# A fused transformer layer on one core: reordering the seam between the output projection and the routed experts

## The reference, cut to what matters

```python
h = rmsnorm(x, norm1_g) * (1 + sc1) + sh1                # the six vectors sh1 .. g2 come from SiLU(cond) @ w_mod + b_mod
p = h @ w_in                                             # two kinds of attention follow; o joins their heads
x = x + g1 * (o @ w_out)                                 # output projection, 2048 x 2048
h2 = rmsnorm(x, norm2_g) * (1 + sc2) + sh2
aff = softmax(h2 @ w_router)                             # 16 experts
gate, idx = top_k(aff.T, cap)                            # each expert picks 64 latent and 16 context tokens
xs = h2[idx]
out = (silu(xs @ w_gate[e]) * (xs @ w_up[e])) @ w_down[e] * gate
x = x + g2 * scatter_add(out, idx)
y = rmsnorm(x, final_norm_g)
```

## Time and profile before

| | |
|---|---|
| median of 3 runs | 2119.72 us (2118.65 to 2121.78) |
| the profiled execution's own time | 2122.72 us |
| its span in the profile | 2120.7 us |
| PE busy | 2033.6 us, 96% |
| DVE busy | 1140.4 us, 54% |
| ACT busy | 478.9 us, 23% |
| GpSimd busy | 162.5 us, 8% |
| DMA | 614.03 MB, mean 290 GB/s |
| mean granted TensorE clock | 0.985 of full speed |

### The profile page before, as it was taken

How to read it: one execution, slowest core, us unless ns; L and a number is a source line. 1 busy time by engine, 2 the same in 40 slices (tenths; PEclk the granted TensorE clock), 3 DMA queues, 4 the chain that set the end, 5 groups by cost and what they waited for, 6 DMA issues and landing times. The chain is left out here.

```text
span 2120.7 us, 37671 instructions
## 1 busy us (share of the span) xinstructions
PE 2033.6 (96%) x15045; PEld 1130.4 (53%) x15045; DVE 1140.4 (54%) x2672; ACT 478.9 (23%) x846; POOL 162.5 (8%) x237
## 2 busy tenths in 40 slices
PE   6999999999999999999969999999999999999994
PEld 3578888787878887888742333333333333333331
DVE  4369988997558877777155333332233333223314
ACT  4232222212257775222110000000000000000003
POOL 1020011111000001111030000000000000000001
PEclk9999999999999999999979999999999999999997
DMA  9956667563120006665379999999999999999997
GB/s 388 410 181 221 218 233 258 190 219 109 60 102 1 2 1 247 218 218 183 111 286 371 405 414 415 417 417 426 419 416 416 416 417 417 426 419 416 418 392 290
DMA packets 71956, 614.03 MB, mean 290 GB/s; under 512 B 8464, under 2 KB 10136, under 8 KB 29136
## 3 DMA queue, kind: packets, MB, share of 16 engines
q1 hardware_dynamic: 47392, 514.36, 58.8%
q0 software_dynamic: 18704, 84.89, 13.1%
q10 hardware_dynamic: 5776, 13.63, 1.8%
HBM read 583.28 MB, written 29.60 MB: 289 GB/s over the span
## 5 line engine op out<-in xcount | busy, mean ns | idle before, releaser
L1249 PE MATMUL ps<-arena 128*32 128x512 f32 x6144 | 664.2, 593 | 0.3 <-DVE arena L2304 0.3
L1249 PEld LDWEIGHTS ps<-arena 128*32 128x32 f32 x6144 | 199.6, 110 | 459.7 <-issue 459.2
L1276 PE MATMUL ps<-arena 128*32 128x512 f32 x3072 | 332.5, 592 | 1.8 <-DVE arena L2315 1.8
L697 PE MATMUL ps<-B_w_hi,B_x_hi 128*128 128x512 f32 x720 | 286.8, 398 | 5.7 <-DVE B_x_lo L2034 3.3
L699 PE MATMUL ps<-B_w_lo,B_x_hi 128*128 128x512 f32 x720 | 281.6, 391 | 0.0
L698 PE MATMUL ps<-B_w_hi,B_x_lo 128*128 128x512 f32 x720 | 281.3, 391 | 0.0
L1276 PEld LDWEIGHTS ps<-arena 128*32 128x32 f32 x3072 | 99.7, 110 | 231.9 <-issue 229.2
L2336 DVE COPY arena<-arena 128x16 f32 x1200 | 157.4, 182 | 100.2 <-issue 99.4
L2312 DVE TENSOR_TENSOR arena<-ps,arena 64x256 f32<-64x256 f32 x96 | 40.0, 417 | 295.4 <-ACT arena L1607 294.8
L1607 ACT ACTIVATE arena<-ps 64x512 f32<-64x512 f32 x48 | 28.6, 595 | 610.3 <-PE ps L1249 610.3
L697 PEld LDWEIGHTS ps<-B_w_hi,B_x_hi 128*128 128x128 f32 x720 | 135.6, 188 | 46.5 <-issue 13.4
(11 more groups left out here) (287 smaller groups left out, 1972.2 us busy)
## 6 DMA issues: line engine op xcount, KB each, us to landing
arena<-in_w_expert SPq DMA_DIRECT2D x192, 2048.0 KB, 13.2
arena<-in_w_in_b SPq DMA_DIRECT2D x36, 1024.0 KB, 5.0
arena<-in_w_mod_q SPq DMA_DIRECT2D x32, 1024.0 KB, 19.2
arena<-in_w_mod POOLq DMA_DIRECT2D x32, 1024.0 KB, 5.4
arena<-in_w_mod POOLq DMA_DIRECT2D x32, 512.0 KB, 4.5
arena<-in_w_out_b SPq DMA_DIRECT2D x16, 1024.0 KB, 6.6
arena<-in_w_mod POOLq DMA_DIRECT2D x64, 256.0 KB, 3.3
arena<-in_x_sample SPq DMA_DIRECT2D x8, 1024.0 KB, 10.4
```

Source lines behind the costliest of these rows:

```text
L697: eng.matmul(out, x_hi, w_hi, start=start, stop=False)
L1249: mm = pe.matmul(bank(g)[32 * q:32 * q + 32, :], e_rows, w[q], start=start, stop=stop, skip_group_check=True)
L1276: mm = pe.matmul(bank(b)[32 * q:32 * q + 32, :], hT[g][:, f, :], w_four[q], start=f == 0, stop=f == 7, skip_group_check=True)
```

## The change

Four edits, all in the seam:

1. The fourth late sum on PE moves from behind block 25 to behind block 26 (LATE_SUM_AT). DVE's copy of the sums out of bank 7 moves from i == 31 to i == 28 and waits for fewer logits. PE's wait for that copy moves from router(3, 0), behind block 31, to router(2, 0), behind block 29.
2. DVE clears its tables at i == 30, ahead of residual(3), instead of behind it. It also writes two small tables (gateC's and idxC's context parts) behind the token numbers instead of ahead of them.
3. ACT alternates squares and copies of the last column block strictly: squares(3, t), take_raw of tile t. Before, the copy was two tiles behind.
4. x1_d gets 16 more columns and holds the factors beside the rows; rstd_d goes. One indirect DMA fetches 2064 columns instead of two that fetch 2048 and 16.

```diff
-LATE_SUM_AT = {7: 0, 13: 1, 19: 2, 25: 3}
+LATE_SUM_AT = {7: 0, 13: 1, 19: 2, 26: 3}
...
-        x1_d = nc.dram_tensor("x1_d", [TOK, D], F32, kind="Internal").ap()
-        rstd_d = nc.dram_tensor("rstd_d", [TOK, ROW_PAD], F32, kind="Internal").ap()
+        x1_d = nc.dram_tensor("x1_d", [TOK, D + ROW_PAD], F32, kind="Internal").ap()
...
                     for pair in ROUTER_AT.get(h, ()):
+                        if (n, pair) == (3, 0):
+                            pe.wait_ge(g2_ready, 1)
                         router(n - 1, pair)
             for t in range(NT):
                 raw_transposes(3, t)
                 if t == 2:
-                    pe.wait_ge(g2_ready, 1)
                     router(3, 0)
...
             for t in range(NT):
                 squares(3, (t,))
-                if t >= 2:
-                    take_raw(3 * NT + t - 2)
-            for t in range(NT - 2, NT):
                 take_raw(3 * NT + t)
...
-            act.wait_ge(gathered, 32)
+            act.wait_ge(gathered, 16)
...
-                pool.dma_start(rstd_d[P * t:P * (t + 1), :], rstdP[:, t, :]).then_inc(r_stored, 16)
+                pool.dma_start(x1_d[P * t:P * (t + 1), D:D + ROW_PAD], rstdP[:, t, :]).then_inc(r_stored, 16)
...
-            for cols, rows in ((slice(0, D), x1_d), (slice(D, D + ROW_PAD), rstd_d)):
-                pool.indirect_dma_start(xs[0:CAP, cols], None, rows[:, :],
-                                        bass.IndirectOffsetOnAxis(ap=idxC[:, 0:1], axis=0)).then_inc(gathered, 16)
+            pool.indirect_dma_start(xs[0:CAP, :], None, x1_d[:, :],
+                                    bass.IndirectOffsetOnAxis(ap=idxC[:, 0:1], axis=0)).then_inc(gathered, 16)
...
-                if i == 31:
+                if i == 28:
                     dve.wait_ge(late_summed, 4)
-                    dve.wait_ge(logits_done, 3 * NT)
+                    dve.wait_ge(logits_done, 2 * NT)
                     dve.tensor_copy(g2rows, bank(7)[:, 3 * P:4 * P]).then_inc(g2_ready, 1)
+                if i == 30:
+                    link(dve.memset(aff32[:, :, :], -1.0))
+                    for m, (a0, v) in enumerate(((0, 0), (2 * NE * 2, 0), (0, 1))):
+                        sel = ident[:, a0:a0 + 4 * NE].rearrange("p (c v e) -> p v e c", c=2, v=2)[:, v]
+                        ins = dve.tensor_reduce(by_kind[:, m, :], sel, AX, ALU.add)
+                    link(ins)
+                    dve.memset(logits_T[64:P, 2 * P:3 * P], 0.0)
                 if h == 7:
                     residual(n)
...
-            link(dve.memset(aff32[:, :, :], -1.0))
...
             dve.tensor_scalar(idxC[CL:CAP, 0:NE], bank(2)[CL:CAP, 0:NE], float(LAT - P), None, ALU.add)
-            dve.tensor_copy(gateC[CL:CAP, :], bank(2)[CL:CAP, NE:2 * NE])
-            dve.tensor_scalar(idxC[0:CX, NE:NE + 1], bank(2)[0:CX, 3 * NE - 1:3 * NE], -float(P), None, ALU.add)
...
             dve.tensor_copy(idxC[0:CL, 0:NE], later).then_inc(cols_ready, 1)
+            dve.tensor_copy(gateC[CL:CAP, :], bank(2)[CL:CAP, NE:2 * NE])
+            dve.tensor_scalar(idxC[0:CX, NE:NE + 1], bank(2)[0:CX, 3 * NE - 1:3 * NE], -float(P), None, ALU.add)
```

More of the change, by code:

```diff
@@ L2407, in _ @@
             dve.wait_ge(con_taken, NE + 1)
-            dve.wait_ge(gathered, 48)
+            dve.wait_ge(gathered, 32)
             for h, taken, at_least in ((0, half_taken, NE), (1, y_taken, NE + 1)):
```

## The result

| | before | after |
|---|---|---|
| median | 2119.72 us (5 runs, 2118.65 to 2121.85) | 2109.13 us (5 runs, 2108.68 to 2110.88) |
| ratio | | 0.9948, 95% interval 0.9937 to 0.9960 |
| profiled execution, its span | 2122.72, 2120.7 us | 2108.68, 2106.9 us |

A forecast was written before the change was run, and what follows sets the result against it. PE was taken to set the pace, so gains in the seam reach the end: -4.3 - 4.1 - 0.6 = -9.0 us, from the profiled 2122.72 to 2113.7, as a median 2110.7; range 2106.5 to 2116.0.

The forecast's parts named there:

- The late sum: Behind block 25: moving the fourth sum behind block 26 removes PE's 2.79 us wait and the half clock; -4.3 us.
- The copy of g2rows and PE's new wait: DVE's copy at i == 28, PE's wait behind block 29: costs nothing, with 13 us of cover.
- The last residual: Around block 31's end: DVE starts it earlier, ACT becomes the limit at 1.30 us a tile, logits come sooner; -4.1 us.
- a rival of -6.5 in all: Last residual: ACT and PE wait for each other under the stricter order, -1.6 instead of -4.1, time 2113.2; 10%.
- The tables and small writes: DVE's four short instructions and two small writes move to places where DVE waited anyway; 0 us.
- The gather: Before the first expert: one DMA instead of two lets ACT's first scaling start earlier; -0.6 us.
- The stores: Rival before the gather: stores drain until 1089 and hold its issue, 1.7 us return, -7.3 in all, 2112.4; 8%.
- The clock at the first expert: Rival: PE's idle gap shrinks by 0.6 us, the first matmuls keep full clock, -1.7 more, 2109.0; 14%.
- the forecast's own case: Whole kernel: the three gains sum to -9.0 us, without the first expert's clock gain; 2110.7 us, 54%.
- the weights as a rival: Experts: weights instead of PE set the pace, so only the -4.3 of PE's blocks counts, 2115.4; 10%.
- The longer rows: Rival at the gather: rows of 8256 bytes are cut into pieces, slower, 2124.9 with 512-byte or 2218 with 64-byte pieces; 4%.

## Why the prediction was right, and where its sizes were off

**The late sum** (-4.3, measured -4.24). The step held, both with the edit alone and with it undone.

**The copy of g2rows and PE's new wait** (cost nothing). Held, with 12.7 us of cover where 13 were stated.

**The last residual** (-4.1, measured -5.49). The mechanism held: DVE is no longer the limit, ACT is. The step of the sum that was mis-sized is the 1.30 us a tile. I added a square's 0.63 to a copy's 0.67, which was half of the 1.33 us of a row of two copies, as if each began where the other ended. In the changed kernel a square begins 0.49 us behind the start of the copy ahead of it and the next copy 0.61 behind the square's: 1.095 a tile, 0.8 us less over four tiles. The 0.4 us for half clock was not due either (granted clock 1.00 in that stage), and the first copy came 0.1 earlier than I had it. I had the strict order as a possible burden, as a rival of -6.5 in all; it is one, of 0.7 us, which the experiment with the old order shows.

**The tables and small writes** (0). Held.

**The gather** (-0.6, -0.34 in this pair, about 0.2 over all the traces). I subtracted two landings of one execution, in which the factors took 4.6 us to land (4.3 and 4.4 in two others), and left the longer single gather at 5.3 us; it took 5.3 to 5.7 in nine executions, the rows alone 5.3 to 5.4 in four. The rule for a DMA's duration that I weighed there (the Trainium skill, DMA: Bandwidth & Descriptors, section Anatomy of one DMA: about 2.0 us plus the bytes at 436 GB/s) would have the factors land first; the traces disagree with it, with 4.3 and 4.6 us for 5 KB, but its result, that merging brings next to nothing, is as near to what was measured as mine.

**The stores** (a rival of 8%, with 1.7 us). They did not decide this result: 1.22 us from the token numbers to the gather. But that is partly luck. The last of the factors landed at 1078.03, which would have let the gather go at 1079.13, and it went at 1079.40; without the chance 0.36 us of the table's third line it would have been held, by 0.1 us. In the six variants of the changed kernel it was 1.32 to 2.30, and with the stores to acc_d out of the way 1.21 and 1.22. In the kernel before the last factors landed at 1089.56 and the gather started at 1091.42, so that with the 1.1 us in between the margin was 0.8 us; the gain itself used it up. I had read the drain of x1's stores from the earlier trace rows; what is waited for is the small stores queued behind them.

**The clock at the first expert** (a rival of 14%, -1.7, measured -1.64). It came true in the profiled execution. The forecast's own case, that the clock stays as it was, did not. The median lies 1.6 us beyond the forecast, just as this rival has it, but that is partly luck. The table differs from the forecast by -2.1 us, which is -1.64 from the clock, -1.39 from the last residual and +0.9 from the small lines. The granted clock of the first 3.4 us of the first expert, before and after:

```profile
1099.29:1102.69 3.40, 3.40 (x20) 0.83 (x24) 0.97 (x4) 2.03 (x3) 0.00 (x0) 0.51 1.07 369
```

```profile
1087.13:1090.53 3.40, 3.40 (x32) 1.06 (x36) 0.97 (x4) 1.85 (x2) 0.00 (x0) 1.00 1.03 330
```

I had reasoned that the gap of idle PE shrinks by 0.6 us, with the gather. It shrank by 1.5, from 2.04 to 0.56, 1.27 of it because the idle multiplications took 7.87 us instead of 6.60: they ran longer at half clock. The stages from 2 us behind their start show it, first of the changed kernel (from 1077.31), then of the kernel before (from 1089.34), with PE alone and the granted clock as the third figure from the right:

```profile
1079.31:1081.31 2.00, 2.00 (x12) 0.50 0.32 45
1081.31:1083.31 2.00, 2.00 (x12) 0.58 0.84 235
```

```profile
1091.34:1093.34 2.00, 2.00 (x16) 0.75 0.25 41
1093.34:1095.34 2.00, 2.00 (x21) 1.00 0.90 254
```

In all thirteen traces the first expert had full clock where the gap was 0.56 to 0.76 (six) and began at half clock where it was 1.46 to 3.72 (seven). That fewer multiplications open the gap and lose the clock in the changed kernel, and more of them close it and win the clock in the kernel before, shows the gap as the cause, one execution for each. Gaps between 0.76 and 1.46 us did not occur. What decides when the clock rises within the multiplications stays open. Six traces are of kernels alike up to there (strict order, copy early). In four of them it rose 5.3 to 5.7 us behind the start of the multiplications, which took 7.69 to 7.87 us for 22. In the other two, the one with 14 and the one with the two gathers (which are issued only later), it rose after 3.6 and 3.4 us, and the 22 of the latter took 6.78. In all other kernels it rose after 2.8 to 3.7 us, and 22 took 6.60 to 6.93. So by these few the changed kernel has the 1.6 us in about two executions of three, and not in every one; the times are too scattered to count them.

**The experts, paced by PE** (the weights as a rival, 10%). Held: what the seam gave reached the end in every trace, less or more what the clock cost or gave: from the first expert's first matmul to the end it was 1019.7 to 1019.9 us, or 1021.1 to 1021.6 with the half clock, whenever the first expert began.

**The longer rows** (a rival of 4%). The gather of 8256-byte rows landed in 5.5 us against 5.3: not cut up.

## What to carry to other kernels

Work that shares a resource with the critical stage (here a PSUM bank) should be taken out before that stage's last block, and a reduction that waits for data from DRAM should stand one block later than its data may come; both cost nothing while the block covers them. Before an order is judged, ask which engine is late in it: ACT's strict order was worth 1.4 us while DVE was late and cost 0.7 us afterwards. A seam that gets shorter also uses up margins that the profile does not show as waits, such as stores that land just in time; look at when each store lands, small ones behind large ones above all. And measure the stretches between fixed instructions, because a gain of 1 us is lost in the scatter of the times.

## What the runs showed of the hardware that I had not expected

- The stretch ahead of any change, from the start to block 25, varied by 5.6 us between executions (1002.5 to 1008.1), while the stretch from the first expert to the end varied by 0.2 us where the first expert had full clock and by 0.5 where it began at half.
- A gap of idle TensorE of 0.56 to 0.76 us kept full clock for what followed, and one of 1.46 us did not, which cost 1.6 us. The same 22 multiplications came out on either side (0.71 and 1.46 us).
- GpSimd's stores of 8 KB took 15.7 to 18.0 us to land behind ten stores of 256 KB, and 6.2 to 8.4 us with five of these moved behind them.
- On ACT a square with its accumulator read starts 0.49 us behind the start of a 0.60 us copy: a rate per tile is to be read from starts in a mixed sequence, not added up from durations.
